# Differential attention: the high-by-low score product on 64 rows, two banks on two halves of the array, q in portions of two tiles

## The reference

```python
def diff_attention(q, k, v, lam, subln_g, lam_init):
    ...
    def block(qblk):
        s = jnp.einsum('bhmqd,bhmkd->bhmqk', qblk.astype(jnp.float32) * scale, kf)
        pr = jax.nn.softmax(s, axis=-1)
        a = pr[:, :, 0] - lam * pr[:, :, 1]
        return jnp.einsum('bhqk,bhkd->bhqd', a, vf)
    ...
    o = rms_norm(o, subln_g, SUBLN_EPS) * (1.0 - lam_init)
    return o
```

## Time and profile before

| | |
|---|---|
| median of three runs | 3203.32 us (3199.81 to 3205.28) |
| span of the profiled execution | 3196.2 us |
| own time of the profiled execution | not listed apart from the three; the median is 7.1 us above the span |
| TensorE busy | 3116.5 us (98%) |
| VectorE busy | 1809.0 us (57%) |
| ScalarE busy | 1553.6 us (49%) |
| GpSimd busy | 1357.8 us (42%) |
| differential stage, first to last score matmul | 564.6 to 1142.3 us |
| granted TensorE clock from 600 to 1140 us | 1.00 |

### The profile page before, as it was taken

One profiled execution on the slowest core, in us unless ns is written; L12 is line 12 of the kernel. 1 busy time (PEld: TensorE's weight loads), 2 busy tenths in 40 slices (PEclk: granted clock), 3 DMA queues, 4 the chain that ended last, 5 costly groups with the idle time before them and its releaser, 6 DMA issues.

```text
span 3196.2 us, 48937 instructions
## 1 busy us (share of the span) xinstructions
PE 3116.5 (98%) x17504; PEld 2695.4 (84%) x17504; DVE 1809.0 (57%) x3106; ACT 1553.6 (49%) x2824; POOL 1357.8 (42%) x1113
## 2 busy tenths in 40 slices
PE   8999999999999999998999999899999999999998
PEld 8988889788888999997887888787778888887887
DVE  5134343898989966665556666666445545552222
ACT  4011110687888878884235555555553334333332
POOL 2123331011111146771245666666576656665222
PEclk9999999999999999999999999999999999999999
DMA  5234336303031348756754775477696678665221
GB/s 168 99 102 131 119 109 177 88 22 87 22 88 31 81 103 198 166 146 192 239 172 158 253 235 172 148 252 249 201 289 197 198 242 259 197 189 194 75 75 56
DMA packets 467407, 493.43 MB, mean 154 GB/s; under 512 B 84064, under 2 KB 377312, under 8 KB 461920
## 3 DMA queue, kind: packets, MB, share of 16 engines
q1 hardware_dynamic: 463824, 484.02, 49.6%
q10 hardware_dynamic: 3344, 6.29, 0.8%
HBM read 322.05 MB, written 168.17 MB: 153 GB/s over the span
## 4 chain that ended last, share of the span: by engine, by line
PE 80%; DMA 6%; POOL 5%; ACT 4%; issue 2%; DVE 1%; SPq 1%; POOLq 0%; ACTq 0%; DVEq 0%
PE c_pv L844 6%; PE h_acc L136 6%; PE h_acc L137 6%; PE h_acc L138 6%; PE a_acc L136 6%; PE a_acc L137 6%; PE a_acc L138 6%; PE b_pv L984 4%; PE c_scores L825 3%; PE c_scores L826 3%; PE c_turned L833 3%; PE b_scores L1236 3%; DMA e_a<-w_up_dram 3%; PE b_turned L1246 2%; PE f_gate_acc L136 2%
## 5 line engine op out<-in xcount | busy, mean ns | idle before, releaser
L2312 POOL TENSOR_TENSOR h_u_lo<-h_u_raw,h_u_hi 128x512 fp32r<-128x512 f32 x224 | 380.2, 1723 | 205.0 <-ACT h_u_hi L2308 204.8
L136 PE MATMUL h_acc<-h_w_hi,h_u_hi 128*128 128x512 f32 x896 | 349.9, 391 | 4.0 <-POOL h_u_lo L2312 2.6
L137 PE MATMUL h_acc<-h_w_lo,h_u_hi 128*128 128x512 f32 x896 | 349.5, 390 | 0.0
L138 PE MATMUL h_acc<-h_w_hi,h_u_lo 128*128 128x512 f32 x896 | 349.3, 390 | 0.0
L741 DVE TENSOR_REDUCE c_neg_half<-c_scores 128x1 f32<-128x1024 f32 x256 | 312.7, 1222 | 44.5 <-PE c_scores L826 44.4
L136 PE MATMUL e_acc<-e_b_hi,e_a_hi 128*128 128x512 f32 x768 | 303.3, 395 | 22.4 <-ACT e_u L2047 17.4
L2402 DVE TENSOR_TENSOR h_h<-h_acc,h_h 128x512 f32<-128x512 f32 x224 | 153.6, 689 | 300.3 <-PE h_acc L138 300.3
L698 ACT ACTIVATE c_e<-c_scores,c_neg_max 128x1024 f32<-128x1024 f32 x256 | 286.3, 1119 | 68.1 <-DVE c_neg_max L748 68.1
L138 PE MATMUL e_acc<-e_b_hi,e_a_lo 128*128 128x512 f32 x768 | 300.7, 392 | 0.0
L137 PE MATMUL e_acc<-e_b_lo,e_a_hi 128*128 128x512 f32 x768 | 300.6, 391 | 0.0
L844 PE MATMUL c_pv<-c_v,c_at 128*128 128x128 f32 x2048 | 270.3, 275 | 0.4 <-ACT c_o L712 0.4
(11 more groups left out here) (204 smaller groups left out, 7867.6 us busy)
## 6 DMA issues: line engine op xcount, KB each, us to landing
h_u_raw<-s_u SPq DMA_DIRECT2D x224, 256.0 KB, 3.5
s_u<-e_u SPq DMA_DIRECT2D x192, 256.0 KB, 3.2
s_qkt<-a_hl SPq DMA_DIRECT2D x128, 256.0 KB, 2.8
e_a<-w_up_dram SPq DMA_DIRECT2D x64, 512.0 KB, 4.7
h_w_raw<-s_t SPq DMA_DIRECT2D x32, 1024.0 KB, 7.9
h_w_raw<-w_down_dram SPq DMA_DIRECT2D x24, 1024.0 KB, 7.8
b_kt<-s_qkt SPq DMA_DIRECT2D x64, 256.0 KB, 9.5
e_t<-w_down_dram SPq DMA_DIRECT2D x32, 512.0 KB, 6.0
```

The source lines that it names most:

```text
L136: nc.tensor.matmul(out, lhs_hi, rhs_hi, start=first, stop=False, skip_group_check=onto)
L137: nc.tensor.matmul(out, lhs_hi, rhs_lo, start=False, stop=False, skip_group_check=onto)
L138: return nc.tensor.matmul(out, lhs_lo, rhs_hi, start=False, stop=last, skip_group_check=onto)
L2312: self.nc.gpsimd.tensor_tensor(self.u_lo[q][s][:], self.u_raw[q][s][:], self.u_hi[q][s][:].bitcast(F32), ALU.subtract).then_inc(self.S["u_ ...
```

## The change

The second score matmul of each bank becomes q high by k low alone, on 64 partitions: the first bank's with partitions 0 to 63 (`qs`), the second bank's with partitions 64 to 127, where a new tile `q_again` holds q high once more. The low-by-low term is no longer computed. In a unit the order is now: both banks' full matmuls, then both banks' 64-row matmuls. To make room for `q_again`, a portion of q is two tiles; loading one takes six transfers of half the size, 32 portions instead of 16.

```diff
-    QT = 4 * P
+    QT, HALF_ROWS = 2 * P, HD
...
         qs = sb("qs", [P, 2, 2, QT], F32R)
+        q_again = sb("q_again", [P, 2, 2, QT], F32R)
...
         def load_q(sp, m):
             if m >= 2:
-                sp.wait_ge(S["scored"], 4 * 4 * (m - 1))
+                sp.wait_ge(S["scored"], 4 * 2 * (m - 1))
             for k in range(4):
                 sp.dma_start(qs[32 * k:32 * k + 32, m % 2].bitcast(F32),
-                             rows(0, m // 4, k % 2, k // 2)[:, :, m % 4 * QT:m % 4 * QT + QT]
+                             rows(0, m // 8, k % 2, k // 2)[:, :, m % 8 * QT:m % 8 * QT + QT]
+                             ).then_inc(q_in[m % 2], 16)
+            for k in range(2, 4):
+                sp.dma_start(q_again[32 * k:32 * k + 32, m % 2].bitcast(F32),
+                             rows(0, m // 8, k % 2, 0)[:, :, m % 8 * QT:m % 8 * QT + QT]
                              ).then_inc(q_in[m % 2], 16)
...
             for n in steps:
-                if n % 4 == 2 and n // 4 + 2 < STEPS // 4:
-                    load_q(sp, n // 4 + 2)
+                if n % 2 == 1 and (n + 3) // 2 < STEPS // 2:
+                    load_q(sp, (n + 3) // 2)
...
                     if u == 0:
-                        pe.wait_ge(q_in[n // 4 % 2], 64 * (n // 8 + 1))
+                        pe.wait_ge(q_in[n // 2 % 2], 96 * (n // 4 + 1))
...
-                    queries = qs[:, n // 4 % 2, m, t % 4 * P:t % 4 * P + P]
+                    toks = slice(t % 2 * P, t % 2 * P + P)
+                    cols = [slice(f * HALF + b * 512, f * HALF + b * 512 + 512) for b in range(2)]
+                    found = [scores[:, (U + 1) % RING * 2 + b] for b in range(2)]
                     for b in range(2):
-                        cols = slice(f * HALF + b * 512, f * HALF + b * 512 + 512)
-                        found = scores[:, (U + 1) % RING * 2 + b]
-                        nc.tensor.matmul(found, queries, kt_hi[h % 2][:, m, cols], start=True, stop=False)
-                        ins = nc.tensor.matmul(found, queries, kt_lo[h % 2][:, m, cols], start=False, stop=True)
+                        nc.tensor.matmul(found[b], qs[:, n // 2 % 2, m, toks], kt_hi[h % 2][:, m, cols[b]],
+                                         start=True, stop=False)
+                    for b in range(2):
+                        rows = slice(b * HALF_ROWS, (b + 1) * HALF_ROWS)
+                        ins = nc.tensor.matmul(found[b], (qs, q_again)[b][rows, n // 2 % 2, m, toks],
+                                               kt_lo[h % 2][rows, m, cols[b]], start=False, stop=True)
                     ins.then_inc(S["scored"], 1)
```

## The result

The changed kernel takes **3251.1 us** (median of four runs, 3246.8 to 3251.6) against 3201.6 for the kernel before (four runs): a ratio of 1.0155, 95% interval 1.0143 to 1.0167. It is slower by 1.55%; 3252 was forecast.

A forecast was written before the change was run, and what follows sets the result against it. The prediction took TensorE's own sequence to bound the differential stage. Row changes +25, queue stalls +22 and clock +2 made +49 on the 3196.2 us span, 3245, and with 7 us around it 3252 us; range 3178 to 3318.

The forecast's parts named there:

- The 7 us that were added to the span: Whole run: the median of runs lay 7.1 us above the profiled span, so 3245 became 3252 us.
- TensorE is the bound of the stage: Differential stage: TensorE's own sequence sets the pace, busy 538.4 of 540 us, 9.05 us a step.
- VectorE's floor: Differential stage: VectorE's work limits how short a step can get, 8.17 us.
- The pair overlaps, two changes of rows cost more than it saves: Each score unit: two changes at 0.167 us less 0.229 saved, +0.105 us, 240 units +25 us.
- The upper end, 0.36 a change: Change of rows, upper bound: full wait 0.167 plus weight load 0.189 us; +0.49 us a unit with overlap.
- The queue: SyncE's queue: q portions issued behind k and v stall iteration 22 and the next head, 11.4 + 10.9 = 22 us.
- The portion behind the first head's k and v: q portion landed by 596, needed by iteration 2 at 598.3: no cost, 2 us of margin.
- The clock: After each q stall the clock may fall, slowing score matmuls: about 1 us per stall, +2 us.
- no gain or loss on the first iterations: First two iterations of the stage: paced by the exponentials, counted as no gain or loss.
- The fast one: Rival: halves overlap and row changes cost nothing (under 0.06 us each); -13 us, 3190 us; chance 0.30.
- That the pair does not overlap: Rival: no overlap within the pair, row changes cost little, only stalls 24 + 2; 3229 us; chance 0.10.
- that weight loads add their full time to a full drain: Rival: change holds back weight load, or drains without overlap; +0.33 to +0.49 a unit, 3303 to 3340 us; chance 0.16.

The follow-up runs named there:

- Only the queue undone: Changed kernel with k and v of heads 2 and 3 issued one transfer a step instead of all at once; 3228.1 us, ratio 1.0086 against the kernel before.
- the grouped kernel: Changed kernel with k, v issued one transfer a step and two units together: four full matmuls, two pairs, then both units' transposes and values; 3443.1 us, ratio 1.0764.
- unpaired 64-row matmuls: Changed kernel with both 64-row matmuls of a unit on partitions 0 to 63, so they can't run at once; 3324.4 us, ratio 1.0384.
- the control of the grouped kernel: Same two-unit order, k and v one transfer a step, but the second product on 128 rows, without any change of rows; 3423.2 us, ratio 1.0697.

## Why the prediction was right

**The number.** Between the medians the loss is 49.5 us, forecast 49; between the two profiled spans, from which the terms were read, it is 53.6. The 7 us that were added to the span mixed two things: a run's time is 1.8 us above its own span (3251.6 and 3249.8), and the rest was the distance of that one execution from the median. That 3252 was met within 1 us is in part luck.

**TensorE is the bound of the stage.** Right: 0.107 us more in a unit came through as +25.7, and with less work on TensorE the step fell to VectorE's floor, 8.17 forecast and 8.19 measured.

**The pair overlaps, two changes of rows cost more than it saves.** Right in the sum: 0.334 forecast for two changes, 0.336 to 0.346 measured (2.37 or 2.38 less 2.263 - 0.229); +25 us forecast, +25.7 measured. The composition was wrong. I had put it that "the next matmul waits until the one before has wholly ended" with its weights loaded meanwhile. The next start comes 0.32 us after the last (0.64 less the 0.32 of the first full matmul), before the modelled end at 0.396, so 0.09 of waiting and not 0.167. And the weight load is not hidden: it starts with its matmul and adds some 0.095 at the change to 64 rows and 0.06 at the change back (0.49 for the transposes in place of 0.43). That the two errors nearly cancel is luck. The upper end, 0.36 a change, counted both to the full and was too dear. The Trainium skill's page TensorEngine Tiling (Array Packing), Key Properties, says that a change of the tiling mode drains the engine. The trace agrees in that each change costs, 0.17 to 0.19 us. Whether the array is quite empty in between, the modelled ends can't tell.

**The queue.** Right, term by term: forecast 29.2 and 28.7 us from k's first issue to the landing of q, measured 28.3 and 28.0 up to TensorE's start (801.17 - 772.86 and 965.09 - 937.12). Forecast stalls 11.4 and 10.9, measured 10.04 and 9.70. One reading was off by a little and changed nothing: the earlier trace rows put the release 23.1 us behind k's first issue and not 23.4. By itself the queue, clock included, is worth 23 us, shown by undoing it, against a forecast of 24. The portion behind the first head's k and v came in time, as forecast: TensorE waits for no q at iteration 2. What the sum left out is the 2.3 us that the old order cost and the new one doesn't.

**The clock.** Mis-sized: forecast 1 us for each stall, measured 2.5 (4.35 and 2.89 in place of 2.37 each). I had counted only the score matmuls as slower, but at the lower level the values of a unit take 1.56 us in place of 0.81 as well.

**Not in the sum:** the stage's start, +3.3 us. I had put no gain or loss on the first iterations. In these two profiles the granted clock from 580 to 590 us is 0.59 where it was 0.92, first the changed kernel, then the one before:

```profile
580.00:590.00 10.00, 9.14 (x28) 4.81 (x28) 8.61 (x13) 6.24 (x12) 0.00 (x0) 0.59 1.00 207
```

```profile
580.00:590.00 10.00, 8.42 (x39) 6.18 (x38) 9.25 (x13) 6.75 (x12) 0.00 (x0) 0.92 1.03 215
```

But that the change did this is not shown. *Only the queue undone* runs the same instructions on TensorE, and on SyncE up to step 20, and it starts iteration 2 at 598.43, where the kernel before had started it:

```profile
598.43 0.71 PE L836 MATMUL c_scores<-c_kt_hi,c_qs 128*128 128x512 f32 x2
```

And 1.7 of the 3.3 us are there before the stage's first score matmul (566.3 against 564.6).

**The rivals.** The fast one fell on its single condition, a change under 0.06 us; it is 0.17 to 0.19. Its estimate of the floor was sound. That the pair does not overlap, and that weight loads add their full time to a full drain, are both refuted by the rows above.

## What to carry to other kernels

Half the rows do not make a matmul shorter; two halves at once do, and here they save one streaming distance (0.23 us at 512 columns). Each change between 64 and 128 rows costs 0.17 to 0.19 us, so a block of 64-row work between full matmuls has to save more than two changes, 0.35 us: with 512 columns, at least two overlapped pairs in a row. In the grouped kernel two pairs saved 0.11 us net on TensorE's stretch (1.33 + 0.49 us against 1.49 + 0.44), but no run here turned that into a faster kernel. And whoever makes loads smaller and nearer to their need should look at what stands ahead of them in their queue: issued behind the 5 MB of a head's k and v, a portion of six 64 KB transfers took 23 us to arrive (778.22 to 801.17).

## What the hardware showed that I had not expected

A weight load that runs under the matmul before, when both have 128 rows and 512 columns, does not do so across a change of rows (its idle 0.36 us with no releaser).

The clock near the stage's start differs from kernel to kernel, at a cost that appears in no wait. With unpaired 64-row matmuls it stayed at the lower level until about 605 us, 25 us after the last wait and with TensorE busy throughout. In the changed kernel it did so to about 588 us. That the 64 rows are the cause is not shown: the control of the grouped kernel, with 128 rows everywhere, still has 0.67 from 580 to 590 and 0.75 from 590 to 600 us. And *only the queue undone*, with the same pairs as the changed kernel, has 0.77 and 0.72 from 570 to 580 and from 580 to 590 us, where the changed kernel has 0.56 and 0.59.

The grouped kernel shows the clock once more: with 1.5 us of idle in every 6.2 us its mean granted clock from 640 to 1300 us was 0.94, and that of its control, with almost the same waits, 1.00. At the full clock its period is the shorter one, 6.24 against 6.28 us; its 29 slow periods make the mean 6.46 against 6.29, 20 us over 122 periods, and that is the difference of the two kernels. Why the clock fell in one and not in the other stays open.
